# The recurrence of a two-layer block: gates one unit later, a third o buffer, spread partition sums, later output weights, first-visit keys scaled on ScalarE

## Chip, cores and metric

The kernel runs on one core of a Trainium2 chip. The metric is device time in microseconds (us) of one execution; a difference of about 0.2% is the smallest that a few runs of this kernel can tell from none.

## What is computed

Two layers of a diffusion-transformer block work on 1024 tokens (a grid of 16 x 64) and a context of 256 tokens, model width 1024. The first layer mixes by windowed means, the second by a bidirectional mLSTM; each mixer is followed by a gated convolutional feed-forward part. The change lies in the second layer's mixer, cut here to what matters:

```python
def _mlstm_chunkwise(q, k, v, ig, lf, state0, with_output):
    b = cumsum(lf)                          # per chunk
    w_end = exp(b_last - b + ig - g_max)
    c_chunk = einsum('bhcsk,bhcsv,bhcs->bhckv', k, v, w_end)     # key_values
    C_new = a * C + e * c_chunk                                   # carry
    s = einsum('bhctk,bhcsk->bhcts', q, k) * d_w                  # scores times decay
    num = einsum('bhcts,bhcsv->bhctv', s, v) + a_t * einsum('bhctk,bhckv->bhctv', q, c_prev)
    h = num / max(abs(den), exp(-m_t))
...
hs = h_f + flip(h_b)                        # forward and backward pass
yx = (sigmoid(o) * hs) @ w_out              # gates, then the output projection
```

There are eight heads, with keys of 64 and values of 128 channels. Everything is fp32; large matmuls are made of three products of high and low parts (fp32r).

## The kernel before, in words

All engines run programs written out by hand, ordered by semaphores; nothing is scheduled by a planner, so the order in the source is the order on each engine.

**Units.** The kernel uses chunks of 128 tokens: 2 of the context and 8 of the grid. A unit is one chunk in one direction; there are 20 (0 to 19), alternately forward and backward. Units 0 to 3 are of the context and only feed the state. Units 4 to 11 are the first visits of the grid's chunks, units 12 to 19 the second visits, which add the other direction's result (`second`). `carried` is 18: units 18 and 19 pass no state on. `again` is 12 to 17, and for these chunks the keys of the first visits (units 6 to 11) are kept in SBUF.

**A unit on TensorE.** In the loop over u from 4 to 19 TensorE issues `front(u + 1)` and `back(u)`. `front` turns the keys of the next unit into PSUM (`keys_turned`, L1768, only for first visits; the bank is free for the next keys once these have been weighed and kept) and makes the scores (L1798). `back(u)` makes the numerator from scores and values (L1857), turns the gated chunk of unit u - 2 (`turn`, L1885), adds the state's part (L1865) and makes the products of keys and values for the state (L1778). The sums of the modulation weights over the partitions (`chunk_columns`, L1898) are matmuls with one column: two chunks' worth after unit 17, six within unit 18, the rest after `turn(18)`. Then the output projection begins (L1122 to L1124), and `turn(19)` stands after its first eighth.

**The other engines in a unit.** VectorE: keys times their weights from PSUM (`kw`, L3819, first visits only), decay times scores (`dmat`, L3825), the new state (`carry`, L3872), the low part of the turned chunk (`g_lo`, L3880), and the division of the numerator (`dens`, `hs`, L3841 to L3861), in that order: front(u + 1), carry(u - 1), turned(u - 2), back(u). ScalarE: the decay's exponentials of unit u + 1, eight instructions (`dmat`, L2802); the copy of the keys to be kept (L2809) or, for units 12 to 17, the kept keys times their weights, head by head (L2819); the high part of the turned chunk of unit u - 2 (`g_hi`, L2792). GpSimd: mask added to the decay rows (`dmat`, L4169), decayed queries (`qa`, L4171), and from unit 14 on the gating of unit u - 2: `hs` times `och` (L4178). SyncE issues the loads: two iterations ahead the decay rows and query factors (L1011, L1014, broadcast to all partitions), the values (L997), and in iteration u the gate values `och` of unit u - 1 (L1023, `gates_in`), into two buffers. Between them stand the loads of the output projection's weights: `mo_raw` in iteration 14, parts of `raw` in iterations 15 and 16 (L1042, L725).

**Who waits for whom.** `turn(u - 2)` waits for the gating (`gated`) and for decay times scores of unit u + 1 (`sd_ready`), since it writes the bank from which VectorE reads the scores. The scores of unit u + 2 wait for `g_lo` of unit u - 2. The numerator of unit u waits bank by bank until VectorE has divided unit u - 1 (`hs_ready`). In `back(18)` the wait for the last state (`state_ready` of 4 * carried) stands ahead of the numerator.

**Earlier in the program.** Before the recurrence the same stretch of code projects o, q, k and v. For the first tile of o, ScalarE takes chunks out of PSUM into two `stage` buffers and stores each to DRAM from its own DMA queue (L2738, L2742). At the same time SyncE issues `res_c` (1 MB, L966), two weight tiles (1 MB each, L719) and two halves of modulation weights (0.5 MB each, L960).

## Time and profile before

| what | value |
|---|---|
| median of 3 runs | 2282.94 us (2279.64 to 2283.0) |
| profiled execution, its own time | 2282.74 us |
| its span, first to last instruction | 2280.9 us |
| TensorE matmul busy | 2201.2 us, 97% of the span |
| weight loads | 1834.1 us, 80% |
| VectorE | 1503.7 us, 66% |
| ScalarE | 1026.2 us, 45% |
| GpSimd | 1023.3 us, 45% |
| mean granted TensorE clock | 0.988 of full speed |

The busy time is a mean over stages. The profile's 40 slices show TensorE at nine tenths or more in nearly all of them. The recurrence of the grid's units runs from 1364 to 1486 us of the span, the output projection follows. In what follows all times are us from the span's start, in that one execution.

### The profile page before, as it was taken

The numbers are of one execution on the slowest core, as the hardware profiler recorded it, in microseconds if no ns is written. First come the engines' busy times: TensorE is split into PE (matmuls) and PEld (weight loads), VectorE is DVE, ScalarE is ACT, GpSimd is POOL, SyncE is SP. The second block draws the span as 40 slices with busy tenths as digits, with TensorE's granted clock in tenths as the row PEclk, the third lists the DMA queues.
The fourth block names the chain that finished last, engine by engine and source line by source line (L and its number), as shares of the span: only waits on it lengthen the run. The fifth ranks groups of instructions, "written<-read, shape, count | busy, mean of one in ns | idle before, by whom it ended". The sixth has DMA issues, their size and how long they took to land.

```text
span 2280.9 us, 35573 instructions
## 1 busy us (share of the span) xinstructions
PE 2201.2 (97%) x13206; PEld 1834.1 (80%) x13206; DVE 1503.7 (66%) x1993; ACT 1026.2 (45%) x1689; POOL 1023.3 (45%) x612
## 2 busy tenths in 40 slices
PE   7988999999999999999999999789999999999997
PEld 5647788888888889998899998767778888888885
DVE  5486666677798835455664727524676777888886
ACT  4654344444444455653433336423554444444443
POOL 0036677777610046661221025530497777771003
PEclk9999999999999999999999999899999999999998
DMA  8764432222292556543431358522212222228352
GB/s 342 252 231 166 157 134 87 83 83 83 84 340 75 167 212 225 191 166 130 124 117 65 107 152 258 175 74 74 75 65 84 82 80 81 108 95 291 129 175 102
DMA packets 123636, 326.33 MB, mean 143 GB/s; under 512 B 11376, under 2 KB 40816, under 8 KB 111216
## 3 DMA queue, kind: packets, MB, share of 16 engines
q1 hardware_dynamic: 105936, 299.35, 38.4%
q10 hardware_dynamic: 17568, 25.17, 3.0%
q8 instruction: 89, 1.46, 0.3%
q14 instruction: 43, 0.35, 0.0%
HBM read 269.82 MB, written 54.66 MB: 142 GB/s over the span
## 4 chain that ended last, share of the span: by engine, by line
PE 90%; DVE 3%; ACT 3%; DMA 2%; issue 1%; POOL 0%; SPq 0%; ACTq 0%; DVEq 0%; POOLq 0%
PE ps L1492 11%; PE ps L1494 11%; PE ps L1493 11%; PE ps L1122 7%; PE ps L1124 6%; PE ps L1123 6%; PE ps L1621 6%; PE ps L1622 6%; PE ps L1623 6%; PE ps L1665 3%; PE ps L1667 3%; PE ps L1666 3%; PE ps L1857 1%; PE ps L1260 1%; PE ps L1396 1%
## 5 line engine op out<-in xcount | busy, mean ns | idle before, releaser
L3225 DVE SCALAR_TENSOR_TENSOR acc<-ps,fcv,acc 128x945 f32<-128x945 f32 (+2 forms) x320 | 391.1, 1222 | 82.2 <-ACT acc L2385 49.6
L3986 POOL TENSOR_TENSOR w_lo<-raw,w_hi 128x2048 fp32r<-128x2048 f32 x36 | 169.5, 4708 | 375.8 <-ACT w_hi L2166 260.6
L4045 POOL TENSOR_TENSOR p_s_lo<-p_s_val,p_s_hi 128x512 fp32r<-128x512 f32 x160 | 242.8, 1527 | 117.1 <-ACT p_s_hi L2329 116.9
L1621 PE MATMUL ps<-da_hi,dw_hi 128*128 128x512 f32 x560 | 218.8, 391 | 0.0
L1622 PE MATMUL ps<-da_hi,dw_lo 128*128 128x512 f32 x560 | 218.1, 389 | 0.0
L1623 PE MATMUL ps<-da_lo,dw_hi 128*128 128x512 f32 x560 | 217.9, 389 | 0.0
L1665 PE MATMUL ps<-w_hi,hx_hi 128*128 128x256 f32 x512 | 145.8, 285 | 3.6 <-ACT stage L2738 3.5
L1666 PE MATMUL ps<-w_lo,hx_hi 128*128 128x256 f32 x512 | 144.9, 283 | 0.0
L1667 PE MATMUL ps<-w_hi,hx_lo 128*128 128x256 f32 x512 | 144.8, 283 | 0.0
L1621 PEld LDWEIGHTS ps<-da_hi,dw_hi 128*128 128x128 f32 x560 | 105.1, 188 | 23.2 <-issue 1.6
L1623 PEld LDWEIGHTS ps<-da_lo,dw_hi 128*128 128x128 f32 x560 | 105.1, 188 | 22.1
L2329 ACT ACTIVATE p_s_hi<-p_s_val 128x512 fp32r<-128x512 f32 x160 | 100.1, 626 | 50.0 <-POOL p_s_val L4036 49.9
L1622 PEld LDWEIGHTS ps<-da_hi,dw_lo 128*128 128x128 f32 x560 | 105.1, 188 | 21.6
L2385 ACT ACTIVATE acc<-ps,fcv 128x1024 f32<-128x1024 f32 x40 | 48.3, 1207 | 154.5 <-DVE ps L3262 148.9
L3669 DVE SCALAR_TENSOR_TENSOR acc_q<-ps,prm,acc_q 128x945 f32<-128x945 f32 (+2 forms) x64 | 78.2, 1222 | 48.9 <-ACT acc_q L2684 46.9
L1665 PEld LDWEIGHTS ps<-w_hi,hx_hi 128*128 128x128 f32 x512 | 98.2, 192 | 4.6 <-issue 2.3
L1122 PE MATMUL ps<-hc_hi,w_hi 128*128 128x256 f32 x352 | 100.2, 285 | 0.6 <-POOL w_lo L3986 0.6
L2166 ACT ACTIVATE w_hi<-raw 128x2048 fp32r<-128x2048 f32 (+1 forms) x62 | 95.3, 1545 | 12.0 <-DMA raw<-in_ffn_w 9.3
L1123 PE MATMUL ps<-hc_hi,w_lo 128*128 128x256 f32 x352 | 99.6, 283 | 0.0
L1124 PE MATMUL ps<-hc_lo,w_hi 128*128 128x256 f32 x352 | 99.5, 283 | 0.0
L1666 PEld LDWEIGHTS ps<-w_lo,hx_hi 128*128 128x128 f32 x512 | 98.2, 192 | 0.1
L1667 PEld LDWEIGHTS ps<-w_hi,hx_lo 128*128 128x128 f32 x512 | 98.2, 192 | 0.0
(523 smaller groups left out, 6499.8 us busy)
## 6 DMA issues: line engine op xcount, KB each, us to landing
f_raw<-in_ffn_w SPq DMA_DIRECT2D x25, 1024.0 KB, 5.0
modw<-in_modw SPq DMA_DIRECT2D x48, 512.0 KB, 8.3
raw<-in_ffn_w SPq DMA_DIRECT2D x23, 1024.0 KB, 5.0
a_scr<-fprod SPq DMA_DIRECT2D x40, 512.0 KB, 2.6
land_w<-in_ffn_w SPq DMA_DIRECT2D x40, 512.0 KB, 4.5
f_raw_b<-in_ffn_w SPq DMA_DIRECT2D x18, 1024.0 KB, 5.0
land_b<-a_scr SPq DMA_DIRECT2D x30, 512.0 KB, 5.4
raw<-in_mlstm_w SPq DMA_DIRECT2D x14, 1024.0 KB, 5.2
```

Source lines behind the costliest of these rows:

```text
L1122: pe.matmul(out, whi, hhi, start=first, stop=False)
L1492: pe.matmul(out, p_hi[p][:, ws], S.x(q, k)[0], start=(k == 0 and name in ("g1", "g2", "s1")), stop=False, skip_group_check=True)
L1493: pe.matmul(out, p_lo[p][:, ws], S.x(q, k)[0], start=False, stop=False, skip_group_check=True)
L1494: mm = pe.matmul(out, p_hi[p][:, ws], S.x(q, k)[1], start=False, stop=(k == KH - 1), skip_group_check=True)
L1621: pe.matmul(out, dw_hi[r][:, ws], da_hi[r][:], start=begins, stop=False, skip_group_check=True)
L1622: pe.matmul(out, dw_lo[r][:, ws], da_hi[r][:], start=False, stop=False, skip_group_check=True)
L1623: mm = pe.matmul(out, dw_hi[r][:, ws], da_lo[r][:], start=False, stop=(i == NK - 1), skip_group_check=True)
L1665: pe.matmul(out, hi[:, k, t0:t0 + CH], wcol(0, k, 0, 2), start=first, stop=False)
L1666: pe.matmul(out, hi[:, k, t0:t0 + CH], wcol(1, k, 0, 2), start=False, stop=False)
L1667: return pe.matmul(out, lo[:, k, t0:t0 + CH], wcol(0, k, 0, 2), start=False, stop=last)
L3225: dve.scalar_tensor_tensor(out, src, cv[:, t:t + 1], out, ALU.mult, ALU.add).then_inc(sem("tap_done"), 1)
L4045: pool.tensor_tensor(p_lo[p][:], src, p_hi[p][:].bitcast(F32), ALU.subtract).then_inc(S.sem("lo_in"), 1)
```

## The change

Seven edits, all in the second layer's mixer:

1. `och` is three buffers instead of two; SyncE issues the gate values of unit u in iteration u (before: of unit u - 1).
2. GpSimd gates unit u - 3 in iteration u instead of unit u - 2, and units 16 to 19 after the last mask.
3. The partition sums stand behind units 12 to 17, two chunks' worth (four matmuls in the program) each.
4. In `back(18)` TensorE waits for the last state only ahead of the state's part.
5. The loads of the output projection's weights move: `raw` parts from iterations 15 and 16 to 17 and 18, `mo_raw` from iteration 14 to behind the loop, once six units are gated. ScalarE waits for eight gatings before it makes `mo_hi`.
6. The keys of units 5 to 11 are weighed by ScalarE, head by head, instead of VectorE.
7. `res_c` is loaded one tile later, once four `stage` copies are done; the second weight tile and the two modulation halves stand behind it.

```diff
-        och = at("och", WORK, [P, 2, 1024])
+        och = [at(f"och{i}", o, [P, 1024]) for i, o in enumerate((WORK, WORK + 4096, WORK + 24576))]
...
-            sp.dma_start(res_c[:], xc_scr).then_inc(sem("resc_in"), 16)
             for t in range(2, len(MSEQ) + 2):
                 K = K_MIN + t
+                if t == 3:
+                    sp.wait_ge(sem("stage_ready"), 4)
+                    sp.dma_start(res_c[:], xc_scr).then_inc(sem("resc_in"), 16)
                 tile_in(K, a["mlstm_w"][t], K % 2)
...
-                    if i >= 2:
-                        sp.wait_ge(sem("gated"), i - 1)
-                    sp.dma_start(och[:, i % 2, :], o_scr[units[u][1] - 2]).then_inc(sem(f"o_in{i % 2}"), 16)
+                    if i >= 3:
+                        sp.wait_ge(sem("gated"), i - 2)
+                    sp.dma_start(och[i % 3][:], o_scr[units[u][1] - 2]).then_inc(sem(f"o_in{i % 3}"), 16)
...
-                if u == 14:
-                    sp.dma_start(mo_raw[:], a["mlstm_w"][len(MSEQ) + 2][:, 0:2048]).then_inc(sem("mo_in"), 16)
-                if u in (15, 16):
-                    tile_out(K_MOUT + u - 15, a["mlstm_w"][len(MSEQ) + u - 15], (K_MOUT + u - 15) % 2)
+                if u in (17, 18):
+                    tile_out(K_MOUT + u - 17, a["mlstm_w"][len(MSEQ) + u - 17], (K_MOUT + u - 17) % 2)
...
-                gates_in(u - 1)
-            gates_in(len(units) - 1)
+                gates_in(u)
+            sp.wait_ge(sem("gated"), 6)
+            sp.dma_start(mo_raw[:], a["mlstm_w"][len(MSEQ) + 2][:, 0:2048]).then_inc(sem("mo_in"), 16)
...
-                    pe.wait_ge(sem("state_ready"), 16 if i == 0 else 4 * carried if u == carried else 4 * (u - 1))
+                    pe.wait_ge(sem("state_ready"), 16 if i == 0 else 4 * (u - 1))
...
                     if u >= 2:
                         turn(u - 2)
+                    if u == carried:
+                        pe.wait_ge(sem("state_ready"), 4 * carried)
...
-                if u == carried - 1:
-                    chunk_columns(0, 2)
-                if u == carried:
-                    chunk_columns(2, 8)
+                if u in again:
+                    chunk_columns(2 * again.index(u), 2 * again.index(u) + 2)
             turn(len(units) - 2)
-            chunk_columns(8, HALVES // 2)
...
             def keep_keys(u):
+                if x_units[0] < u < again[0]:
+                    dr, n = units[u]
+                    act.wait_ge(sem("kt_done"), u + 1)
+                    act.wait_ge(sem("unit_done"), u - 1)
+                    for h in range(HEADS):
+                        c = 32 * dr + h
+                        ins = act.activation(kw[u % 2][:, 64 * h:64 * h + 64], ps[:, keys_bank(u), 64 * h:64 * h + 64], ACT.Copy,
+                                             scale=cols[:, n, 1, c:c + 1])
+                    ins.then_inc(sem("kw_ready"), 1)
                 if u in kept_index:
-                    act.wait_ge(sem("kw_ready"), u + 1)
...
+            act.wait_ge(sem("gated"), 8)
             act.wait_ge(sem("mo_in"), 16)
...
-                if u < again[0]:
+                if u <= x_units[0]:
                     dve.wait_ge(sem("kt_done"), u + 1)
...
-                for v in ([u - 2] if u < len(units) - 1 else [u - 2, u - 1, u]):
+                for v in ([u - 3] if u < len(units) - 1 else [u - 3, u - 2, u - 1, u]):
                     if v in sec_index:
                         i = sec_index[v]
                         pool.wait_ge(sem("hs_ready"), 3 * (x_index[v] + 1))
-                        pool.wait_ge(sem(f"o_in{i % 2}"), 16 * (i // 2 + 1))
-                        pool.tensor_tensor(hs[:, units[v][1] - 2, :], hs[:, units[v][1] - 2, :], och[:, i % 2, :], ALU.mult).then_inc(sem("gated"), 1)
+                        pool.wait_ge(*gate_landed(i))
+                        pool.tensor_tensor(hs[:, units[v][1] - 2, :], hs[:, units[v][1] - 2, :], och[i % 3][:], ALU.mult).then_inc(sem("gated"), 1)
```

GpSimd at units 14 to 16, before: `dmat` and `qa` of unit 14, then the gating of unit 12, and so on.

```order
158 L4169 TENSOR_TENSOR dmat<-dmat,masks 128x1024
159 L4171 TENSOR_TENSOR qa_168<-qa_168,q_x 128x512
160 L4169 TENSOR_TENSOR dmat<-dmat,masks 128x1024
161 L4171 TENSOR_TENSOR qa_169<-qa_169,q_x 128x512
162 L4178 TENSOR_TENSOR hs<-hs,och 128x1024
163 L4169 TENSOR_TENSOR dmat<-dmat,masks 128x1024
164 L4171 TENSOR_TENSOR qa_170<-qa_170,q_x 128x512
165 L4178 TENSOR_TENSOR hs<-hs,och 128x1024
```

The same place now; rows 160 and 161 are again unit 14.

```order
160 L4182 TENSOR_TENSOR dmat<-dmat,masks 128x1024
161 L4184 TENSOR_TENSOR qa_169<-qa_169,q_x 128x512
162 L4182 TENSOR_TENSOR dmat<-dmat,masks 128x1024
163 L4184 TENSOR_TENSOR qa_170<-qa_170,q_x 128x512
164 L4191 TENSOR_TENSOR hs<-hs,och_178 128x1024
165 L4182 TENSOR_TENSOR dmat<-dmat,masks 128x1024
```

The mask of unit 15 now stands ahead of the gating of unit 12, and so on for each later unit.

TensorE at the end of the recurrence, before: numerator, turn and state's part of units 18 and 19 with the partition sums between them (each `x2` row is one chunk's two matmuls).

```order
6281 L1898 MATMUL ps<-ones,msum_324 128x1 x2
6282 L1898 MATMUL ps<-ones,msum_325 128x1 x2
6283 L1798 MATMUL ps<-q_x,k_x 128x128 x8
6284 L1857 MATMUL ps<-vch_171,dmat 128x129 x8
6285 L1885 MATMUL ps<-ident,hs 128x128 x8
6286 L1865 MATMUL ps<-state,qa_169 128x129 x8
6287 L1898 MATMUL ps<-ones,msum_326 128x1 x2
6288 L1898 MATMUL ps<-ones,msum_327 128x1 x2
```

The same place now, from the last sums of unit 17 to the projection's first matmul.

```order
6291 L1905 MATMUL ps<-ones,msum_pair_325 128x1 x2
6292 L1905 MATMUL ps<-ones,modm_320 128x1 x2
6293 L1803 MATMUL ps<-q_x,k_x 128x128 x8
6294 L1862 MATMUL ps<-vch_171,dmat 128x129 x8
6295 L1892 MATMUL ps<-ident,hs 128x128 x8
6296 L1872 MATMUL ps<-state,qa_169 128x129 x8
6297 L1862 MATMUL ps<-vch_173,dmat 128x129 x8
6298 L1892 MATMUL ps<-ident,hs 128x128 x8
6299 L1872 MATMUL ps<-state,qa_170 128x129 x8
6300 L1892 MATMUL ps<-ident,hs 128x128 x8
6301 L1127 MATMUL ps<-g_hi,w_hi 128x512
```

Nothing stands between units 18 and 19 any more, nor behind `turn(18)`.

SyncE at the first tile of o, before: the loads that follow the first two modulation halves.

```order
241 L966 DMA res_c<-xc_scr 128x2048
242 L719 DMA raw<-in_mlstm_w 128x2048 x2
243 L960 DMA modm_318<-in_modw 128x1024
244 L960 DMA modm_319<-in_modw 128x1024
```

The same now; row 242 waits for four `stage` copies.

```order
241 L723 DMA raw<-in_mlstm_w 128x2048
242 L974 DMA res_c<-xc_scr 128x2048
243 L723 DMA raw<-in_mlstm_w 128x2048
244 L964 DMA modm_320<-in_modw 128x1024
245 L964 DMA modm_321<-in_modw 128x1024
```

One tile keeps its place; three loads stand behind `res_c`, and `res_c` behind the wait.

## Rows read from the trace of the kernel before

**Rows 1.** Busy time by stretch: start:end, length, each engine, clock, DMA share, GB/s.
```profile
1385.90:1414.25 28.35, 28.35 (x339) 24.98 (x340) 23.75 (x69) 17.14 (x57) 17.96 (x10) 1.00 0.82 231
1414.25:1455.00 40.75, 33.30 (x377) 29.20 (x378) 29.70 (x98) 24.14 (x82) 27.21 (x14) 0.96 0.97 288
1470.00:1480.00 10.00, 10.00 (x67) 9.71 (x67) 3.95 (x14) 3.88 (x3) 2.35 (x1) 0.67 0.01 2
```
**Rows 2.** Waits, 1350 to 1500: waiter <- releaser, us in total, times, longest.
```profile
POOL hs L4178 <- DMA och<-o_scr: 13.0, 4, 5.5
DVE dmat L3825 <- ACT dmat L2802: 8.0, 5, 3.4
```
**Rows 3.** Timeline of TensorE: start, us, operation, in brackets idle before.
```profile
1426.76 2.05 PE L1857 MATMUL ps<-vch,dmat 128*128 128x129 f32 x16
1432.41 1.67 PE L1885 MATMUL ps<-ident,hs 128*128 128x128 f32 x8 [3.60 <-DVE dmat L3825]
...
1449.79 1.06 PE L1885 MATMUL ps<-ident,hs 128*128 128x128 f32 x8 [1.04 <-issue]
...
1460.66 1.05 PE L1898 MATMUL ps<-ones,msum 128*128 128x1 f32 x8
1461.64 1.16 PE L1798 MATMUL ps<-q_x,k_x 64*128 64x128 f32 x16
1466.17 3.16 PE L1857 MATMUL ps<-vch,dmat 128*128 128x129 f32 x16 [3.37 <-DVE state L3872]
...
1475.16 3.79 PE L1857 MATMUL ps<-vch,dmat 128*128 128x129 f32 x16
...
1486.54 0.50 PE L1122 MATMUL ps<-g_hi,w_hi 128*128 128x512 f32 x1 [0.69 <-DVE g_lo L3880]
...
1501.92 0.66 PE L1260 MATMUL ps<-sq_p,ones 128*32 128x128 f32 x8 [5.07 <-ACT sq_p L2098]
```
**Rows 4.** Timeline of GpSimd at units 12 to 15.
```profile
1423.86 2.36 POOL L4178 TENSOR_TENSOR hs<-hs,och 128x1024 f32<-128x1024 f32 x1 [5.50 <-DMA och<-o_scr]
1426.17 2.36 POOL L4169 TENSOR_TENSOR dmat<-dmat,masks 128x1024 f32<-128x1024 f32 x1
```
**Rows 5.** Timeline of ScalarE: decays, kept keys, weighed keys.
```profile
1371.13 4.78 ACT L2802 ACTIVATE dmat<-dmat,cols 128x128 f32<-128x128 f32 x16
...
1388.70 0.60 ACT L2809 ACTIVATE kept_keys<-ps 128x512 f32<-128x512 f32 x1 [1.55 <-DVE kw L3819]
1389.19 2.43 ACT L2802 ACTIVATE dmat<-dmat,cols 128x128 f32<-128x128 f32 x8
...
1415.39 2.02 ACT L2819 ACTIVATE kw<-kept_keys,cols 128x64 f32<-128x64 f32 x8 [0.77 <-PE ps L1778]
```
**Rows 6.** DMA issues, 1410 to 1510: count, KB each, median us to landing.
```profile
qa<-query_scr SPq DMA_DIRECT2D x11, 128.0 KB, 6.5
...
raw<-in_mlstm_w SPq DMA_DIRECT2D x2, 512.0 KB, 10.5
```
**Rows 7.** Timeline of VectorE within one unit of the second visits.
```profile
1443.77 1.22 DVE L3880 TENSOR_TENSOR g_lo<-ps,g_hi 128x1024 fp32r<-128x1024 f32 x1 [1.22 <-ACT g_hi L2792]
...
1445.67 2.16 DVE L3853 SCALAR_TENSOR_TENSOR hs<-ps,dens,hs 128x128 f32<-128x128 f32 x8
1448.47 1.22 DVE L3825 TENSOR_TENSOR dmat<-dmat,ps 128x1024 f32<-128x1024 f32 x1 [0.64 <-ACT dmat L2802]
...
1451.95 1.22 DVE L3880 TENSOR_TENSOR g_lo<-ps,g_hi 128x1024 fp32r<-128x1024 f32 x1 [1.22 <-ACT g_hi L2792]
```
**Rows 8.** Timeline of three engines at the first tile of o.
```profile
1044.43 0.35 PE L1665 MATMUL ps<-w_hi,hx_hi 128*128 128x256 f32 x1 [1.95 <-ACT stage L2738]
...
1043.90 0.38 ACT L2738 ACTIVATE stage<-ps 128x256 f32<-128x256 f32 x1 [7.05 <-DMA o_scr<-stage]
...
1032.31 0.91 SPq L719 DMA_DIRECT2D raw<-in_mlstm_w  x2
```
**Rows 9.** One tile's instructions, `stage`: time from issue to landing of its stores.
```profile
DMA to landing us min/median/max: 1.8/2.2/8.8
```

4 lines of the change are left out of this document (3 added, 1 removed), and 2 rows, old and new, of the table shared.

## The prediction

> **What bounds the kernel now.** I read the page first: TensorE is busy for 97% of the span of 2280.9 us, so only its idle time and its slow time can be won, some 80 us in all. The busy time by stretch splits the recurrence in two. In the first visits TensorE is busy for all of 28.35 us (units 7 to 11, 5.79 us each with keys to turn, 5.20 without), while the 16 DMA engines are 0.82 taken; from 1414 to 1455 it is busy for 33.3 of 40.75 us and the DMA engines are 0.97 taken [rows 1]. Then the waits: GpSimd waited 13.0 us for gate values and VectorE 8.0 us for ScalarE's decays [rows 2]. In the timelines both are one chain, seen once in full: the gating of unit 12 starts at 1423.86, 5.50 us late, the mask of unit 15 behind it at 1426.17 [rows 4], and TensorE stands 3.60 us before `turn(12)` at 1432.41 [rows 3]. At the end it waits 3.37 us for the last state and then runs slowly: the numerator of unit 19 takes 3.79 us where that of unit 14 took 2.05 [rows 3], with the granted clock at 0.67 in that stretch [rows 1], between the levels of 1.2 and 2.4 GHz. The projection starts at 1486.54 [rows 3].
>
> **The change, part by part.** I work out when the projection starts; after it both kernels do the same.
>
> *Keys on ScalarE.* VectorE is rid of one instruction a unit, but TensorE has no gap there [rows 1], so this gains nothing. ScalarE gets eight instructions, 2.02 us as for the kept keys, beside a decay of 2.43 and a copy of 0.60 [rows 5]: 5.05 us of 5.79. These read PSUM, where the row reads SBUF. At the start the keys of unit 5 stand behind its decay: 1371.13 + 4.78 / 2 + 2.02 = 1375.5, where TensorE wants them at 1375.3 (two units of 5.79 ahead of 1386.9, where a unit starts). With the semaphore's delay: +0.35 us. Bounds: 0, and what 0.60 us for each of the eight would make of it, the copy's time for eight times the columns (a rival below).
>
> *Partition sums.* Eight records took 0.98 us (1460.66 to 1461.64 [rows 3]). Behind units 12 and 13, where TensorE has no gap, they cost 2 x 0.98 = +1.96. Behind 14 to 17 they fall into waiting, as follows.
>
> *Unit 14.* `turn(12)` needs the gate values, the gating, and decay times scores of unit 15. The values are issued one iteration (5.2 us) earlier and no `mo_raw` lies beside them; the mask of unit 15 no longer stands behind the gating. Its rows had landed by 1426.17, when its mask began without a wait [rows 4]; at the median of 6.5 us from issue [rows 6] they landed by about 1422, since SyncE issues them once the numerator of unit 11 is done, at 1414.25 (where the first stretch of rows 1 ends). Mask 2.36, queries 1.3 and gating 2.36 end at 1428 (or 1432.2 by the late bound, +1.1); decay and product are earlier. The numerator of unit 14 starts at 1426.76 + 1.96 + 0.35 = 1429.1 and takes 1.98; so `turn(12)` is at 1431.05, not 1432.41. The 3.60 us are gone, the 2.31 added in front remain.
>
> *Units 15 to 17: a loop takes over.* From `turn` to the end of `g_lo` takes 1449.79 to 1451.95 + 1.22 = 1453.17, 3.38 us [rows 3, 7]. Then VectorE divides: from 1444.99 to 1447.83, 2.84 us; then decay times scores, 1.22, and small gaps of 0.1 bring the next `turn` 4.15 us after `g_lo` [rows 7]. The period is 3.38 + 4.15 = 7.55 us. Before it was 8.18 (`g_lo` at 1443.77 and 1451.95), of which 0.64 was the wait for the decay [rows 7]; that goes. TensorE's own work is 5.20, a turn of 1.07 and 0.98 for the sums, 7.25, so the sums are hidden here. GpSimd's work (6.0) fits too. DMA: 28.35 x 0.82 / 5 = 4.65 us a unit without gate values; the second stretch took 39.5 us for 5.5 such units and 5.2 MB of other loads, so 2.7 us a MB and 1.4 for a unit's gate values [rows 1]; 6.05 a unit, 7.5 where a part of `raw` comes. The DMA engines follow, just.
>
> `g_lo` of unit 12 ends at 1434.4, that of 15 three periods later at 1457.1; the scores of unit 19 start 0.8 later (7.25 less scores 1.09 and numerator 1.98 is 4.18 after the turn, less 3.38), 1457.9, where they started at 1461.64: **-3.7**, with all sums done.
>
> *Units 18 and 19.* The numerator of 18 no longer waits for the state (3.37). `turn(16)` 1457.1 + 4.15 = 1461.25; `g_lo` 1464.6; now the numerator of 19 waits for the division of 18 (its first heads 1.7 us after `g_lo`): 1466.35, `turn(17)` 1468.3, `g_lo` 1471.7, `turn(18)` 1471.8, `g_lo` 1475.2. **Projection at 1475.3, -11.2 us.** The low part of its first weights (VectorE, behind `g_lo` of 17) fits between. The new wait of 2.9 us at unit 19 stands where 24 records of sums stood.
>
> *Clock.* That wait is shorter than the two (3.60, 3.37) behind which the trace shows slow matmuls: after the first only a turn (1.67 for 1.06), after the second a numerator (3.16 for 2.05) as well [rows 3]. Bounds: 0 to +2.4 (a numerator at 3.7 and a turn at 1.7). I take the middle, **+1.1**: the length of the wait is near theirs, but only two blocks can be caught.
>
> *Output weights.* The parts of `raw` are issued around 1435 and 1443, at 10.5 us to land [rows 6]; wanted at 1463 and later. `mo_raw` goes out once unit 17 is gated, about 1462, and lands before 1475; it is wanted behind `turned(19)`, some 20 us after its issue. Covered; if not, each us late is a us lost. The stall of 5.07 us in the projection's second eighth, where TensorE waits for ScalarE's work behind `mo_hi` [rows 3], is not touched.
>
> *`res_c`.* TensorE waited 1.95 us at 1044.43 for a `stage` copy, which waited 7.05 for a store to land; median is 2.2 [rows 8, 9]. Ahead of the store SyncE had issued `res_c` and two tiles, up to 1032.31 + 0.91 [rows 8]. Now one tile is there, so the store lands before the copy is wanted: **-1.95**. The later loads meet the next stores, which TensorE needs 6 us later; bounds 0 and -1.95, and I take the full gain since the wait has that slack. `res_c` itself was used 50 us later. The rule against it: the Trainium skill, "DMA: Bandwidth & Descriptors", section "Queues, rings and completion order", says that each DMA engine takes turns between the queues packet by packet. By that ScalarE's store would not stand behind SyncE's backlog, this part would give 0 and the time would be 1.95 us longer; the 7.05 against 2.2 speaks for the backlog.
>
> Sum: -11.2 (with +0.35 and +1.96 inside) + 1.1 - 1.95 = -12.0. The profiled execution took 2282.74 in all, 1.8 around the span, and lies 0.2 below the median of 2282.94; so 2282.94 - 12 = **2271.0**.
>
> **Rivals.**
> *Half of it.* Something of the chain mask, decay, product stays late, because the DMA engines at 6 to 7.5 us a unit fall behind: then unit 14 keeps its 3.60 and the period its 8.18 (3 x 0.64), together 5.5 to 6 of the 12. For it: 6.5 and 10.5 us to landing with the engines full [rows 6]. Against: two iterations of lead, and 2 MB gone. Time 2277.
> *Given back in the projection.* Its start is earlier, but `mo_raw` or the modulation columns come late, or the stall behind `mo_hi` grows by as much. If all 10.1 us of the recurrence go, only `res_c` is left: 2281. Against: the loads land over 10 us ahead of their use, by the above.
> *ScalarE binds the first visits.* At 0.60 us for each of the eight, a unit takes 4.8 + 2.43 + 0.60 = 7.8 us instead of 5.79, six times, and unit 5's keys come 2.8 us later: +15, time 2271 + 15 = 2286. It costs from 0.34 us each, and eats the gain from 0.55. Against: 2.02 for eight [rows 5].
> *The clock falls within the second visits, slower than before.* Now TensorE has three short waits in each of units 15 to 17 and one-column matmuls between. If the clock stayed at its lower level there, a unit would take about 5 us more (numerator 3.7 for 2.0, and all others alike), from unit 14 to 19 +25: 2271 + 25 = 2296. It decides once 2.4 units run so. Against: the second stretch had waits of over 1 us in each unit and was granted 0.96 [rows 1]; eight such records stood ahead of scores at full speed, 1.16 [rows 3]. The Trainium skill, "TensorE: Matmul & The Clock Gate", section "A second HAM failure mode: psum-queue depth-cycling", tells of a kernel whose frequent short idles between groups made the clock swing; that speaks for this rival, and the trace so far does not show it.
>
> **How the numbers follow.** Forecast (2268 to 2274): 0.66. Half: 0.17. Given back: 0.06. ScalarE binds: 0.04. Clock: 0.03. What I have not seen and leaves the time as it is: 0.04. The difference that a measurement can tell is 0.2%, 4.6 us. Faster: the first two, and a part of the third, 0.85; same: 0.10; slower: 0.05. The range goes from 2268 (no clock loss, and a run as far below its median as one of those shown) to 2278, which takes in the half.
>
> **What would show it.** Right: no idle before `turn(12)`; `g_lo` every 7.5 to 7.6 us; scores of 19 about 3.7 us earlier relative to unit 12; idle of about 3 us before the numerator of 19, released by VectorE's `hs`; all L1905 sums by then; the projection 11 to 13 us earlier in the span; no wait near 1044. Wrong: ScalarE over 5.8 us a unit in the first visits; GpSimd waiting for `och` or rows from unit 15 on; a granted clock under 0.9 from 1430 to 1460; idle above 5 us in the projection's second eighth.

## The result, and the profile of the kernel after

The changed kernel takes 2268.25 us (median of 4 runs, 2266.68 to 2268.69); the kernel before 2281.29 (4 runs, 2279.26 to 2283.0). The ratio is 0.994, 95% interval 0.9924 to 0.9955: 13.0 us less, where I had forecast 12.0 less and 2271.0. The time lies 2.75 below the forecast and 0.25 above the lower end of the range that I gave (2268 to 2278). 1.65 of the 2.75 is the reference: the three runs that I started from had their median at 2282.94, and a fourth at 2279.26 moved it to 2281.29. Some 1.1 is the change itself. A second comparison (run e11 below, 5 runs against 9) gives 2268.17 against 2279.99, ratio 0.9947 (0.9932 to 0.9962), 11.8 less. So the forecast gain of 12.0 lies between the two measured ones, 13.0 and 11.8; that its parts were not all right is shown further down.

Of the profiled execution (2268.69 us, span 2266.6) I read the timeline of TensorE at the places of [rows 3].

```profile
1037.35 0.39 ACT L2742 ACTIVATE stage<-ps 128x256 f32<-128x256 f32 x1 [1.47 <-DMA o_scr<-stage]
...
1044.60 0.38 ACT L2742 ACTIVATE stage<-ps 128x256 f32<-128x256 f32 x1 [3.24 <-DMA o_scr<-stage]
...
1047.75 0.39 ACT L2742 ACTIVATE stage<-ps 128x256 f32<-128x256 f32 x1 [2.77 <-DMA o_scr<-stage]
...
1050.22 0.39 ACT L2742 ACTIVATE stage<-ps 128x256 f32<-128x256 f32 x1 [2.08 <-DMA o_scr<-stage]
...
1051.62 0.32 PE L1139 MATMUL ps<-sq_c,ones 128*32 128x64 f32 x8 [0.92 <-ACT sq_c L2060]
```

These are the copies of the first tile of o [rows 8], in ScalarE's timeline, and the one wait in TensorE's. The 7.05 us before the third copy are 1.47, and the 1.95 us before TensorE's matmul are gone. The copies behind it wait instead (3.24, 2.77, 2.08; the waits at the same place before were at most 1.15), since `res_c` and its followers are now issued from 1038.60 on. So ScalarE reaches the squares `sq_c` only 0.24 us earlier than before, counted from the first matmul of o (29.87 for 30.11), while TensorE comes 1.95 earlier, and it stands 0.92 us where it did not stand before.

TensorE in the recurrence, lines of numerator (L1862), turn (L1892) and projection (L1127):

```profile
1426.70 2.05 PE L1862 MATMUL ps<-vch,dmat 128*128 128x129 f32 x16
1428.59 1.04 PE L1892 MATMUL ps<-ident,hs 128*128 128x128 f32 x8
...
1436.01 1.06 PE L1892 MATMUL ps<-ident,hs 128*128 128x128 f32 x8 [0.20 <-issue]
...
1458.33 0.85 PE L1892 MATMUL ps<-ident,hs 128*128 128x128 f32 x6 [0.20 <-issue]
...
1463.40 2.07 PE L1862 MATMUL ps<-vch,dmat 128*128 128x129 f32 x16 [2.91 <-DVE hs L3866]
...
1472.25 0.60 PE L1127 MATMUL ps<-g_hi,w_hi 128*128 128x512 f32 x1 [2.37 <-DVE g_lo L3893]
...
1487.34 0.66 PE L1265 MATMUL ps<-sq_p,ones 128*32 128x128 f32 x8 [4.81 <-ACT sq_p L2102]
```

Against [rows 3]: no idle before `turn(12)` (3.60 before), a turn every 7.44 us (8.17 from `turn(13)` to `turn(14)` before, its start 1441.62 and 1449.79), one wait of 2.91 before the numerator of unit 19 and that numerator at 2.07 (3.79), the stall in the projection as it was (4.81 for 5.07). Busy time by stretch, columns as in [rows 1]:

```profile
1383.94:1412.29 28.35, 28.35 (x338) 24.98 (x340) 21.38 (x65) 23.91 (x90) 18.34 (x11) 1.00 0.75 222
1412.29:1453.04 40.75, 40.16 (x458) 36.19 (x460) 32.79 (x106) 26.05 (x86) 33.15 (x17) 1.00 1.02 302
```

The first visits are as full as before, and ScalarE has gone from 17.14 to 23.91 us in them. In the second stretch (as long as that of [rows 1], from the same point of the loop) TensorE is busy for 40.16 us instead of 33.30, in full. GpSimd waits no more for gate values. In place of the waits of [rows 2] there are these (behind the colon: us in total, times, longest), counted here from 1340 to 1500:

```profile
POOL dmat L4182 <- DMA qa<-query_scr: 66.1, 14, 29.7
...
POOL hs L4191 <- DVE hs L3866: 17.7, 3, 8.1
...
DVE dmat L3838 <- ACT dmat L2806: 5.1, 2, 4.5
```

Counted alike, GpSimd waited 59.4 us in 10 times for queries before; the longest, 29.7 us now and 28.8 before, is one wait ahead of the loop.

**A table by stretch.** Executions of one kernel differ by up to 5 us before the changed part begins, so I compare lengths between the same instructions: the first matmul of the first tile of o, the turned keys of unit 5, with which the loop of the units begins (the texts written ahead of the runs e10 to e13 call the same instruction the keys of unit 6), `turn(12)`, and the projection's first matmul. These are the first two in the kernel before:

```profile
1022.16 0.28 PE L1665 MATMUL ps<-w_hi,hx_hi 128*128 128x256 f32 x1
...
1369.50 0.66 PE L1768 MATMUL ps<-ident,k_x 128*128 128x128 f32 x4 [0.47 <-ACT stage L2738]
```

and in the kernel after:

```profile
1021.19 0.28 PE L1670 MATMUL ps<-w_hi,hx_hi 128*128 128x256 f32 x1
...
1367.54 0.66 PE L1773 MATMUL ps<-ident,k_x 128*128 128x128 f32 x4 [0.47 <-ACT stage L2742]
```

| us | o to keys of 5 | keys of 5 to turn(12) | keys of 5 to projection | numerator of 19 | all, us |
|---|---|---|---|---|---|
| before | 347.34 | 62.91 | 117.04 | 3.79 | 2282.74 |
| after | 346.35 | 61.05 | 104.71 | 2.07 | 2268.69 |
| e1: edit 7 alone | 345.59 | 63.98 | 117.49 | 3.79 | 2280.97 |
| e2: without edit 6 | 345.87 | 61.05 | 106.09 | 2.62 | 2267.83 |
| e3: sums in the waits | 346.08 | 59.39 | 104.51 | 3.53 | 2268.28 |
| e4: without edit 4 | 345.70 | 61.05 | 112.77 | 3.78 | 2274.24 |
| e5: without edit 2 | 345.90 | 61.55 | 107.79 | 3.78 | 2273.75 |
| e6: two buffers | 345.75 | 61.05 | 104.72 | 2.07 | 2268.85 |
| e7: edit 5 alone | 348.81 | 63.63 | 113.93 | 2.06 | 2278.08 |
| e8: edit 2 alone | 348.70 | 59.39 | 107.76 | 2.07 | 2274.92 |
| e9: projection's order | 345.97 | 61.05 | 106.22 | 2.74 | 2262.54 |
| e10: e9 and e3 | 345.68 | 59.40 | 104.69 | 3.46 | 2261.38 |
| e11: after, again | 346.25 | 61.05 | 106.09 | 2.61 | 2268.17 |
| e12: without edit 3 | 345.79 | 59.39 | 104.43 | 3.42 | 2266.93 |
| e13: after, gap filled | 345.89 | 61.05 | 104.70 | 2.16 | 2267.06 |
| e14: e9, gaps filled | 345.78 | 61.05 | 104.70 | 2.16 | 2260.56 |
| e15: e10, gaps filled | 346.39 | 59.38 | 103.06 | 2.16 | 2259.92 |

The last column is one execution for before, after and e1 to e8, a median of 4 or 5 from e9 on. The lengths are of one execution each. Before against after: 1.0 less up to the keys, 12.3 less in the recurrence, and nothing from the projection's start to the end (794.36 and 794.35, although the stall there is 0.3 shorter). A further 0.97 of the span's 14.3 lies ahead of the first matmul of o, where nothing was changed: such starts lie between 1019.11 (e7) and 1024.47 (e5). So the last column of two single executions can differ by 5 us without a cause in the edits, and I read e1 to e8 by the lengths.

### The profile page after: what moved, and what is told of

Its sections match the earlier page's. It is cut to its first block, busy times and chain, and to the rows that moved or that the text cites. A ratio compares the mean times of both kernels' runs of the same rounds, so it can differ in the third digit from the quotient of the medians.

```text
span 2266.6 us, 35623 instructions
## 1 busy us (share of the span) xinstructions
PE 2195.4 (97%) x13206; PEld 1828.9 (81%) x13206; DVE 1503.4 (66%) x1986; ACT 1036.8 (46%) x1745; POOL 1023.8 (45%) x612
## 3 DMA queue, kind: packets, MB, share of 16 engines
q8 instruction: 89, 1.46, 0.3%
## 4 chain that ended last, share of the span: by engine, by line
PE 91%; DVE 3%; ACT 3%; DMA 2%; issue 1%; POOL 0%; ACTq 0%; SPq 0%; DVEq 0%
PE ps L1497 11%; PE ps L1499 11%; PE ps L1498 11%; PE ps L1127 7%; PE ps L1128 6%; PE ps L1129 6%; PE ps L1626 6%; PE ps L1627 6%; PE ps L1628 6%; PE ps L1670 3%; PE ps L1672 3%; PE ps L1671 3%; PE ps L1862 1%; PE ps L1265 1%; PE ps L1401 1%
## 5 line engine op out<-in xcount | busy, mean ns | idle before, releaser
L1127 PE MATMUL ps<-hc_hi,w_hi 128*128 128x256 f32 x352 | 100.2, 285 | 0.7 <-POOL w_lo L3999 0.7
L4259 POOL TENSOR_TENSOR y_x<-y_x,res_x 128x512 f32<-128x512 f32 x12 | 17.1, 1451 | 180.7 <-DVE y_x L3964 180.7
```

Of the source, the lines that this page charges most:

```text
L1127: pe.matmul(out, whi, hhi, start=first, stop=False)
```

## The experiments

**e1, edit 7 alone**, in the kernel before.

```diff
-            sp.dma_start(res_c[:], xc_scr).then_inc(sem("resc_in"), 16)
             for t in range(2, len(MSEQ) + 2):
+                if t == 3:
+                    sp.wait_ge(sem("stage_ready"), 4)
+                    sp.dma_start(res_c[:], xc_scr).then_inc(sem("resc_in"), 16)
```

> The kernel before with edit 7 alone (res_c, one weight tile and two modulation halves behind four stage copies). Backlog theory: ScalarE's second pair of stage copies no longer waits 7.05 us for a store, TensorE's wait of 1.95 us near 1044 is gone, and everything from there on starts 1.95 us earlier: the projection at 1484.6, the time about 2281 beside 2282.9. Rival, the DMA engines take turns between the queues: store and wait stay as they were, the projection at 1486.5.

The wait near 1044 is gone, and o to keys is 1.75 shorter. The recurrence kept its length (117.49), but the wait before `turn(12)` grew to 4.67. So the backlog on the other queue did hold the store, and part of the gain is given back behind the loads in their new place: TensorE waits 0.36 us for the squares `sq_c` here too.

**e2, edit 6 undone**: VectorE weighs the keys again.

```diff
-                if x_units[0] < u < again[0]:
-                    ...
-                        ins = act.activation(kw[u % 2][:, 64 * h:64 * h + 64], ps[:, keys_bank(u), ...], ACT.Copy, scale=...)
...
-                if u <= x_units[0]:
+                if u < again[0]:
                     dve.wait_ge(sem("kt_done"), u + 1)
```

> The changed kernel with edit 6 undone: VectorE weighs the keys of units 5 to 11 again. Theory that the edit gives nothing: TensorE is packed in the first visits either way, units of 5.79 us, the projection at 1472.2 within 0.2 us, time as the changed kernel's. Rival, it was VectorE's relief that removed a late division or a late product at the turn from first to second visits: a wait of 0.3 to 1 us shows before a numerator of units 11 to 13, and the projection is later by as much.

Up to `turn(12)` the two are equal to 0.01 us. Edit 6 brings and costs nothing that can be seen. The difference to the projection is the numerator of unit 19, which ran slowly in this execution.

**e3, the sums only where TensorE waits**: none behind units 12 and 13, the missing four chunks' worth between units 18 and 19.

```diff
-                if u in again:
-                    chunk_columns(2 * again.index(u), 2 * again.index(u) + 2)
+                if u in again[2:]:
+                    chunk_columns(2 * again.index(u) - 4, 2 * again.index(u) - 2)
+                if u == carried:
+                    chunk_columns(8, HALVES // 2)
```

> The changed kernel with the partition sums of units 12 and 13 taken away from there: two chunks' worth behind each of units 14 to 17, the last four behind unit 18, where TensorE waits 2.91 us for VectorE. Theory of the waits: 1.96 us of sums leave the packed units 12 and 13 and vanish in the wait; the projection starts 1.9 to 2.0 us earlier, 1470.3. Clock theory: a wait of 1 us instead of 2.91 keeps the clock as it is, no effect. Rival, DMA or decays had no slack in units 12 to 14 and the 1.96 us covered them: a wait of up to 2 us comes before turn(12) and nothing is gained.

`turn(12)` comes 1.66 us earlier, but the projection only 0.2. In TensorE's timeline:

```profile
1458.64 1.50 PE L1905 MATMUL ps<-ones,msum_pair 128*128 128x1 f32 x12
1460.00 0.58 PE L1905 MATMUL ps<-ones,modm 128*128 128x1 f32 x4
1461.62 3.53 PE L1862 MATMUL ps<-vch,dmat 128*128 128x129 f32 x16 [1.03 <-DVE hs L3868]
```

The gap has shrunk from 2.91 to 1.03 us, and the numerator behind it is slower than in the kernel after, 3.53 for 2.07. The numerator starts 1.65 us earlier (counted from the keys of unit 5) and takes 1.46 longer: what was won ahead is lost at the lower clock.

**e4, edit 4 undone**: in unit 18 the wait for the last state stands ahead of the numerator again.

```diff
-                    pe.wait_ge(sem("state_ready"), 16 if i == 0 else 4 * (u - 1))
+                    pe.wait_ge(sem("state_ready"), 16 if i == 0 else 4 * carried if u == carried else 4 * (u - 1))
...
-                    if u == carried:
-                        pe.wait_ge(sem("state_ready"), 4 * carried)
```

> The changed kernel with edit 4 undone: in back(18) the wait for the last state stands ahead of the numerator again. Theory: the numerator of 18 starts at carry's end (about 1459.3) instead of 1456.1, turn(16) at 1461.2 instead of 1458.3, the projection 2.9 us later, 1475.2, if the clock stays. Clock theory: a wait of about 3.2 us is as long as those behind which the kernel before ran slowly (3.37, 3.60), longer than the 2.91 that stayed at full speed; then numerators take over 3 us, and the projection is 4 to 6 us later.

```profile
1457.94 3.78 PE L1862 MATMUL ps<-vch,dmat 128*128 128x129 f32 x16 [3.37 <-DVE state L3883]
...
1467.34 3.78 PE L1862 MATMUL ps<-vch,dmat 128*128 128x129 f32 x16 [2.91 <-DVE hs L3864]
```

Two waits and two slow numerators: the recurrence is 8.1 us longer than in the profile of after, more than either theory had. Counted from the keys, the numerator of 18 starts 3.4 us later, that of 19 5.5 later, the projection 8.1 later. The last 2.5 are the numerator and turn of unit 19 at the lower clock, which e5 shows with edit 4 in place (2.6). So some 5.5 us belong to edit 4, the largest share of any edit that was undone alone: 3.4 of waiting and 2.1 of lower clock behind it.

**e5, edit 2 undone**: GpSimd gates unit u - 2 again.

```diff
-                for v in ([u - 3] if u < len(units) - 1 else [u - 3, u - 2, u - 1, u]):
+                for v in ([u - 2] if u < len(units) - 1 else [u - 2, u - 1, u]):
```

> The kernel after with edit 2 undone: GpSimd gates unit u-2 in iteration u again, so the mask and the decayed queries of unit 15 stand behind the gating of unit 12 (edits 1, 3 to 7 stay). Theory 1 (the 3.60 us before turn(12) were the late gate values; once they are loaded an iteration earlier the order on GpSimd hardly matters): the gating starts without a DMA wait once unit 12 is divided; its hs ends at about 1421 in the kernel after, gating 2.36, mask 2.36, decay 2.43, product 1.22 would end at 1429.5, so turn(12) waits 1 us at most, the period stays at 7.4 to 7.5, and the projection starts within 0.5 us of 1472.3. Theory 2 (the order on GpSimd was half of the gain, as my prediction told it): turn(12) waits 2 us or more on the decay, the period is over 7.8, the projection starts at 1474 or later.

```profile
1431.92 1.06 PE L1892 MATMUL ps<-ident,hs 128*128 128x128 f32 x8 [0.33 <-POOL hs L4191]
...
1439.36 1.06 PE L1892 MATMUL ps<-ident,hs 128*128 128x128 f32 x8 [0.20 <-issue]
```

GpSimd's mask of unit 15 in the same run, and VectorE's one wait for a decay between 1400 and 1500:

```profile
1425.69 2.35 POOL L4182 TENSOR_TENSOR dmat<-dmat,masks 128x1024 f32<-128x1024 f32 x1
...
DVE dmat L3838 <- ACT dmat L2806: 1.1, 1, 1.1
```

`turn(12)` waits 0.33 us, and the period behind it is 7.44. The bracket names GpSimd's gating, but that is the gating of unit 13, which `turn(12)` does not need; that of unit 12 had ended at 1425.73. What `turn(12)` waited for is again the chain mask, decay, product: the mask of unit 15 at 1425.69, straight behind the gating, ScalarE's decay at 1428.07 behind it, and VectorE's product, 1.08 us late, from 1430.55 to 1431.77. So in time the run is as theory 1 has it, half a us to `turn(12)`, but the wait is small because the sums of edit 3 stand ahead of it: `turn(12)` comes 61.55 us after the keys, where e8 and e12, with the other order on GpSimd and no sums there, have 59.39. What the order is worth with the loads moved and without those sums was not run; the two lengths put it near 2.2 us. The other 2.6 us of the longer way to the projection are the numerator and turn of unit 19 at the lower clock.

**e6, gate values as if there were two buffers.**

```diff
-                    if i >= 3:
-                        sp.wait_ge(sem("gated"), i - 2)
+                    if i >= 2:
+                        sp.wait_ge(sem("gated"), i - 1)
```

> The kernel after, but the gate values of unit v wait until all but one of the earlier ones are used up, as with two buffers (edit 1 half undone: still issued an iteration earlier in SyncE's order). SyncE is in order, so with gating at u-3 this load waits for the gating of unit v-2, and what stands behind it (decay rows and queries of the coming units) waits as well. Theory 1 (the third buffer is what allows edit 2): GpSimd waits for rows or gate values by 1 us or more in units 15 to 17, the period rises over 7.7, the projection starts 1 to 4 us after 1472.3. Theory 2 (the lead of two iterations has room for it): same period, projection within 0.3 us of 1472.3.

No difference in the recurrence (61.05 to `turn(12)`, 104.72 in all). The third buffer is not needed.

**e7, edit 5's loads alone**, in the kernel before.

```diff
-                if u == 14:
-                    sp.dma_start(mo_raw[:], ...)
-                if u in (15, 16):
-                    tile_out(K_MOUT + u - 15, ...)
+                if u in (17, 18):
+                    tile_out(K_MOUT + u - 17, ...)
...
             gates_in(len(units) - 1)
+            sp.wait_ge(sem("gated"), 6)
+            sp.dma_start(mo_raw[:], ...)
```

> The kernel before with edit 5's loads alone: mo_raw behind the loop, the raw parts in iterations 17 and 18. Theory 1 (the 1 MB of mo_raw and the parts of raw delayed the gate values through the full DMA engines): the wait of GpSimd for the gate values of unit 12 shrinks from 5.50 to about 3 us or less (1 MB at 2.7 us), the 3.60 us before turn(12) to 1 or less; the projection starts 2 to 4 us before 1486.54. Theory 2 (the gate values come late since they are issued late, behind the broadcasts of the next unit): the 5.50 and the 3.60 stay within 1 us, the projection starts within 1 us of 1486.54.

```profile
1423.01 2.36 POOL L4178 TENSOR_TENSOR hs<-hs,och 128x1024 f32<-128x1024 f32 x1 [6.14 <-DMA och<-o_scr]
...
1431.55 1.94 PE L1885 MATMUL ps<-ident,hs 128*128 128x128 f32 x8 [4.32 <-DVE dmat L3825]
```

Half of each theory. At unit 12 nothing is won (6.14 and 4.32 where it was 5.50 and 3.60), and in the kernel before SyncE had issued those gate values at 1416.44, ahead of `mo_raw` at 1417.13: they were late because they were issued late. The later ones landed in time: from `turn(12)` to `turn(15)` it is 23.78 us instead of 25.13 (1432.41 to 1457.54). The rest of the 3.1 us, 2.5, is the numerator and turn of unit 19, which ran at full clock here, and that right behind the same one-column sums as in the kernel before:

```profile
1470.02 2.39 PE L1898 MATMUL ps<-ones,msum 128*128 128x1 f32 x20
1472.27 0.58 PE L1898 MATMUL ps<-ones,msum_pair 128*128 128x1 f32 x4
1473.00 2.06 PE L1857 MATMUL ps<-vch,dmat 128*128 128x129 f32 x16
```

**e8, edit 2 alone**, in the kernel before.

```diff
-                for v in ([u - 2] if u < len(units) - 1 else [u - 2, u - 1, u]):
+                for v in ([u - 3] if u < len(units) - 1 else [u - 3, u - 2, u - 1, u]):
```

> The kernel before with edit 2 alone: GpSimd gates unit u-3 in iteration u, two buffers, gate values issued late. Theory 1 (the chain mask, decay, product behind the gating made the wait): the mask of unit 15 runs by 1423, decay and product no longer hold turn(12), which then waits only for the gating, 1423.9 or later + 2.36 = 1426.2 to 1428.7; the 3.60 us shrink to 0 to 1. But SyncE, which waits for a gating before it refills a buffer, is held up one unit more, so gate values and rows come late from unit 15 on and the projection is 0 to 3 us earlier than 1486.54. Theory 2 (the late gate values are the cause whatever the order): turn(12) still waits 2.5 us or more.

No wait before `turn(12)`, period 7.44, 9.3 of the 12.3 us of the recurrence, by one line; some 2.5 of the 9.3 are the numerator and turn of unit 19, which ran at full clock in this execution (2.07 for 3.79), as in e7. Even so it is more than theory 1 expected: SyncE was not held up, GpSimd's masks waited 2.52, 1.25 and 1.20 us for rows, and ScalarE waited at most 0.8 us for a mask. Gate values that came late did no harm here with an iteration between them and their use. So the order on GpSimd takes the wait before `turn(12)` away with the loads as they were; the loads without it (e5) shorten the same wait, with the sums of edit 3 covering most of what is left. Behind `turn(12)` either gives the period of 7.44.

**e9, another order in the projection**, in the kernel after: ScalarE squares the first eighth before it makes the next high parts, and TensorE sums these squares later.

```diff
-                        if k == 2 and d >= 1:
+                        if k == (6 if (h, d) == (0, 1) else 2) and d >= 1:
                             half_sums("p", 2 + h, d - 1)
...
+            copy_out(0, 0)
             for n in range(4):
                 plain_high(0, n)
-            for d in range(KT):
+            for d in range(1, KT):
                 copy_out(0, d)
```

> The kernel after with two steps of the output projection in another order: ScalarE takes the first eighth out of PSUM and squares it before it makes the four high parts of the next weights, and TensorE sums those squares behind the seventh of the eight channel blocks of the second eighth instead of behind the third. In the kernel after, TensorE stands 4.81 us before these sums (released by ScalarE's sq_p) and its next 12 matmuls take 0.63 us instead of 0.39. Theory 1 (ScalarE's order alone makes the stall, and the slow matmuls follow from the idle): both go, 4.8 + 12 x 0.2 = 7.2 us less from the projection's start to the second half's first squares; 2261 us in all. Theory 2 (another wait takes its place: the squares wait for GpSimd's w_lo, which ends at 1482.97, or the later high parts hold up GpSimd): part of it stays, 2263 to 2267. Theory 3 (all given back later): 2268.

2262.54 us, ratio to before 0.9919 (0.9904 to 0.9934), 5.6 us less than the kernel after beside it. The stall is gone:

```profile
1487.96 0.42 PE L1265 MATMUL ps<-sq_p,ones 128*32 128x128 f32 x8
```

From the projection's start to the end of the program it is 787.3 us instead of 793.4 in e11 (794.4 in the first profile), 6.1 to 7.1 less, near the 7.2 of theory 1. Which of the two moves, ScalarE's or TensorE's, does it was not taken apart.

**e10, e9 with the sums of e3.**

> As the run above, and with the sums of the run e3 (none behind units 12 and 13, the missing ones between units 18 and 19). In e3 the end of the recurrence was reached only 0.2 us earlier (104.51 against 104.71 us from the keys of unit 6), since the numerator of unit 19 ran slowly. Theory 1 (the clock at unit 19 is a matter of chance, whatever stands in the gap): this run is 0 to 3 us faster than the one above, about 2260. Theory 2 (one-column matmuls in the gap bring the slow clock every time, a true wait of 2.9 us only sometimes): same as the run above within 1 us, the numerator of unit 19 slow again.

2261.38 us, ratio 0.9918 (0.9903 to 0.9933), within the scatter of e9. The numerator of unit 19 is slow again (3.46 behind 1.04 of idle time), as theory 2 has it for this run; its "every time" does not hold, since the numerators of e7 and e8 behind such sums took 2.06 and 2.07.

**e11, the kernel after again.**

> The kernel after, unchanged, as the measure for the runs beside it: 2268 us, ratio 0.994. Theory 1 (the clock at unit 19 is a matter of chance): the numerator of unit 19 behind its 2.9 us of idle time may be fast (2.07) or slow (up to 3.8) in this execution; from the keys of unit 6 to the projection 104.7 us if fast, 107.7 if slow. Theory 2 (2.9 us of idle are always short enough): 104.7 again.

```profile
1462.49 2.61 PE L1862 MATMUL ps<-vch,dmat 128*128 128x129 f32 x16 [2.91 <-DVE hs L3866]
1464.90 1.91 PE L1892 MATMUL ps<-ident,hs 128*128 128x128 f32 x8
```

The same code behind the same 2.91 us of idle time, and here numerator and turn run slowly where the first profile had 2.07 and 1.07: 1.4 us more to the projection. The clock is a matter of the execution.

**e12, edit 3 undone**: the sums as before.

```diff
-                if u in again:
-                    chunk_columns(2 * again.index(u), 2 * again.index(u) + 2)
+                if u == carried - 1:
+                    chunk_columns(0, 2)
+                if u == carried:
+                    chunk_columns(2, 8)
             turn(len(units) - 2)
+            chunk_columns(8, HALVES // 2)
```

> The kernel after with edit 3 undone: the partition sums stand as before (two chunks' worth behind unit 17, six between units 18 and 19, the rest behind turn(18)). Theory 1 (the sums behind units 12 and 13 are pure cost, 1.96 us, the others are free in either place): from the keys of unit 6 to turn(12) 59.4 us instead of 61.05, period 7.44, no idle before the numerator of unit 19, whose clock decides: 102.8 us to the projection if it stays up, about 106 if it falls; in all 2266 or 2269. Theory 2 (the sums keep TensorE's clock up in units 14 to 17): without them granted clock under 0.95 there and a period over 7.5, 2270 or more.

```profile
1458.79 2.39 PE L1905 MATMUL ps<-ones,msum 128*128 128x1 f32 x20
1461.04 0.80 PE L1905 MATMUL ps<-ones,msum_pair 128*128 128x1 f32 x4
1461.77 3.42 PE L1862 MATMUL ps<-vch,dmat 128*128 128x129 f32 x16
```

Same as the kernel after or a little better (0.9941, interval 0.9926 to 0.9957, against 0.9947). 24 one-column matmuls fill the gap without a rest, and the numerator still takes 3.42. Edit 3 brings nothing.

**e13, the gap filled**: the kernel after with 20 transposes of 128 columns ahead of the numerator of unit 19, into a bank that nobody reads (work is added, none left out).

```diff
+            def fill(n0):
+                for j in range(n0):
+                    pe.transpose(ps[:, 7, P * (j % 3):P * (j % 3) + P], k_tile(2, j % 4), ident[:])
...
+                    if u == carried + 1:
+                        fill(20)
                     for g, heads in enumerate(by_bank):
```

> The kernel after, with 20 transposes of 128 columns whose results nobody reads, put into the wait ahead of the numerator of unit 19 (some 2.6 of the 2.91 us; they add work and leave none out). Theory 1 (the clock at unit 19 falls because TensorE stands there; whether it does is decided by chance at 2.91 us): with the gap filled the numerator takes 2.05 every time, from the keys of unit 6 to the projection 104.7 us or less (106.1 and more in four of six profiles with the gap open), 2267 us in all. Theory 2 (the clock falls there for another reason, such as the waits from unit 15 on taken together): the numerator still takes 2.6 us or more, 2268 or more.

```profile
1458.86 2.40 PE L1845 MATMUL ps<-ident,k_x 128*128 128x128 f32 x20
1461.74 2.16 PE L1869 MATMUL ps<-vch,dmat 128*128 128x129 f32 x16 [0.48 <-DVE hs L3873]
```

The numerator runs at full clock, and in e14 and e15 too (2.16 each). The time, 2267.06 (2265.8 to 2269.79), cannot be told from that of the kernel after: the stake is 1 us. By chance, three profiles of three would be fast about once in forty times, if four in fourteen are (the table without e13 to e15).

**e14, e9 with three gaps filled** (20 ahead of the numerator of 19, 8 ahead of `turn(18)`, 16 behind it).

> The run e9 with such transposes in three waits: 20 ahead of the numerator of unit 19, 8 ahead of turn(18), 16 behind it, ahead of the projection. Theory 1: numerator, turn and the projection's first nine matmuls (0.63 us each in the kernel after, 0.40 at full clock) all run at full clock, 1.4 + 9 x 0.2 = 3.2 us less than e9, 2259 to 2260. Theory 2: same as e9, 2262.5.

```profile
1468.02 1.91 PE L1845 MATMUL ps<-ident,k_x 128*128 128x128 f32 x16
1470.56 0.50 PE L1127 MATMUL ps<-g_hi,w_hi 128*128 128x512 f32 x1 [0.63 <-DVE g_lo L3903]
...
1476.77 1.09 PE L1899 MATMUL ps<-ident,hs 128*128 128x128 f32 x8 [0.43 <-POOL hs L4201]
...
1483.58 0.43 PE L1265 MATMUL ps<-sq_p,ones 128*32 128x128 f32 x8 [0.93 <-ACT sq_p L2111]
```

The projection's first matmuls take 0.40 instead of 0.63, but TensorE then meets `turn(19)` 0.43 and the squares 0.93 too early: of the 1.8 us hoped for there, 0.4 is left by these waits, and 0.2 by the length from the projection's start to the end (787.0 for 787.3 in e9), less than two executions of one kernel differ by. 2260.56 us, ratio 0.9913 (0.99 to 0.9927), 2.0 less than e9 was in its own comparison; the intervals of the two overlap.

**e15, e10 with gaps filled**: the last four chunks' sums and four transposes stand behind `turn(18)`, 20 and 8 transposes ahead as in e14. Against e14, behind the loop:

```diff
             fill(8)
             turn(len(units) - 2)
-            fill(16)
+            chunk_columns(8, HALVES // 2)
+            fill(4)
```

> As the run above, but no sums behind units 12 and 13 (1.66 us less to turn(12)); the last four chunks' sums (one-column matmuls) stand behind turn(18) with four transposes, where the run above has sixteen transposes. Theory 1 (one-column matmuls do not keep the clock up, transposes do): numerator of unit 19 at 2.05, the projection's first matmuls slow again (0.63); 1.66 less than the run above and up to 1.8 more: 2259 to 2260. Theory 2 (any matmul keeps it up): all fast, 2257.5 to 2258.

```profile
1468.54 1.40 PE L1912 MATMUL ps<-ones,msum_pair 128*128 128x1 f32 x12
1469.80 0.58 PE L1912 MATMUL ps<-ones,modm 128*128 128x1 f32 x4
1470.24 0.64 PE L1845 MATMUL ps<-ident,k_x 128*128 128x128 f32 x4
1471.08 0.50 PE L1127 MATMUL ps<-g_hi,w_hi 128*128 128x512 f32 x1 [0.20 <-DVE g_lo L3904]
1471.89 0.60 PE L1127 MATMUL ps<-g_hi,w_hi 128*128 128x512 f32 x1
```

2259.92 us, ratio 0.9909 (0.9894 to 0.9924), 20.4 less than before: the lowest median, not to be told from e14. With the clock kept at unit 19, what the sums behind units 12 and 13 cost does come back: 103.06 us to the projection instead of 104.70. TensorE rested for only 0.20 us ahead of the projection, and yet its matmuls are slow from the second on (0.60, then 0.63), where e14, with transposes in place of the sums, has 0.40. Theory 1, on one profile of each.

## Why the prediction was right or wrong

**The chain before `turn(12)`: right.** Idle 3.60 gone; keys of 5 to `turn(12)` took 61.05, forecast 61.55 (1431.05 - 1369.50). The chain mask, decay, product that I named is what binds in e5 too. But I told it as the sum of three edits, and it is not: e8 has it by the order on GpSimd alone, and e7 shows that the loads of the output weights had no part in it, since these gate values had been issued ahead of `mo_raw`. e5 has most of it by the earlier gate values, with the sums covering the rest.

**The sums behind 12 and 13: right** (+1.96 forecast). 1.66 came back when they were moved away (e3, e12), since `turn(12)` then waits a little. What I missed is that they buy nothing: without them at units 12 and 13, the gap at unit 19 holds them, at the same end time. Only with transposes in that gap (e15) does their cost of 1.66 show in the end time as well.

**Keys of unit 5: the term was over by 0.35.** I took 2.02 us for ScalarE's eight, the row from SBUF, and my working (1375.5 against 1375.3) gave 0.2 of the 0.35; for the semaphore's delay that made up the rest I had no row. From PSUM the eight took 1.70 to 1.79, and the keys of units 5 and 6 stood 5.78 us apart, as before. One row of them:

```profile
1385.59 1.75 ACT L2817 ACTIVATE kw<-ps,cols 128x64 f32<-128x64 f32 x8
```

**The period: right in mechanism, over in size.** 7.44 for 7.55, four times, 0.44 us. (My two terms, 3.38 and 4.15, add up to 7.53.) From `turn` to the end of `g_lo` it is 3.37 us, as forecast (3.38). From there (1438.16 + 1.22) to the next `turn` at 1443.45 it is 4.07, not 4.15: the small gaps of 0.1 that I had put between VectorE's steps are not there. VectorE's timeline behind that `g_lo`:

```profile
1440.06 2.16 DVE L3866 SCALAR_TENSOR_TENSOR hs<-ps,dens,hs 128x128 f32<-128x128 f32 x8
1442.13 1.21 DVE L3838 TENSOR_TENSOR dmat<-dmat,ps 128x1024 f32<-128x1024 f32 x1
1445.60 1.23 DVE L3893 TENSOR_TENSOR g_lo<-ps,g_hi 128x1024 fp32r<-128x1024 f32 x1 [1.22 <-ACT g_hi L2796]
```

**Units 18 and 19: right.** The new wait was forecast at 2.9 and released by `hs`; it is 2.91. From `turn(16)` to the projection it took 13.92, forecast 14.05 without the clock's share.

**The clock, +1.1: 0 in the first profile, right on the average.** In the six profiles that have the open gap of 2.91 us (after, e2, e5, e6, e9, e11) the way to the projection is longer than 104.71 by 0, 1.38, 2.58 (e5, less the 0.5 at `turn(12)`), 0.01, 1.51 and 1.38: 1.14 on average. That it is the standing that brings the lower clock was only argued before; e13, e14 and e15 are the evidence for it: with matmuls of 128 columns in the gap the numerator took 2.16 in three of three.

**`res_c`, -1.95: the step that failed.** "The later loads meet the next stores, which TensorE needs 6 us later": I looked for the next reader of PSUM, and put the new place of the loads at nothing. The first to suffer was ScalarE's own queue of work: three copies waited 8.1 us together, the squares behind them came only 0.24 us earlier, and TensorE stood 0.92 us there. All fourteen profiles with edit 7 have this wait, of 0.36 to 0.92 us; the three without it have none. So of the 1.95 us of waiting, 1.0 to 1.6 are saved, and 1.0 in the pair of profiles.

A second thing, which I had not priced, works the other way. Behind the old wait the matmuls ran slowly in two of the three profiles that have it (e7 and e8; 0.41 us where 0.28 is usual):

```profile
1041.37 0.36 PE L1665 MATMUL ps<-w_hi,hx_hi 128*128 128x256 f32 x1 [1.94 <-ACT stage L2738]
...
1042.49 0.41 PE L1665 MATMUL ps<-w_hi,hx_hi 128*128 128x256 f32 x1
```

The granted clock was 0.91 in the 20 us around that wait in both, and TensorE was busy for 344.7 and 344.8 us from o to the keys instead of 343.3; none of the fourteen with edit 7 has it (343.1 to 343.4, granted 1.00). So the length from o to keys is 347.3, 348.8 and 348.7 without edit 7 and 345.9 on average with it, 2.4 less: some 1.3 of waiting and 1.1 of clock. That this comes near the 1.95 is luck.

I had weighed a rule against this step. The Trainium skill, "DMA: Bandwidth & Descriptors", section "Queues, rings and completion order", says that each DMA engine takes turns between the queues packet by packet. From it I had worked out that the store would not stand behind another queue's backlog. The wait of 7.05 that fell to 1.47 when the backlog was moved (1.36 in e1, with this edit alone) speaks against its giving 0 here.

**Together.** Recurrence -10.1 forecast, -12.3 in the profile, -11.2 with the clock's average. Without the clock's share that is -11.2 forecast and -12.3 measured: `turn(12)` 0.5 earlier, the period's 0.46, and 0.13 in units 18 and 19. `res_c` -1.95 forecast, -1.0 in the profile, -2.4 against the mean of the three; from the projection's start on, nothing. In the one pair of profiles the two errors have opposite signs, which is why the sum looks better than its parts. The rest of the miss in the absolute time is the reference: medians of the kernel before were 2282.94, 2281.29, 2279.99 and 2280.33, and I gave a range of 3 us downwards from a median of three.

**The rivals.** None came. Half of it: GpSimd found its gate values (waits gone), though the DMA engines were full. Given back in the projection: the stall shrank by 0.3, and from the projection's start to the end both took 794.4. ScalarE in the first visits: 5.79 us a unit, unchanged. The clock within the second visits: granted 1.00 from 1412 to 1453 in spite of a 0.20 us wait and one-column matmuls in each unit. The Trainium skill, "TensorE: Matmul & The Clock Gate", section "A second HAM failure mode: psum-queue depth-cycling", tells of a kernel in which short idles between groups made the clock swing; that does not show here.

What stays open: why the same 2.91 us cost nothing in two executions and 1.4 to 2.6 us in four, why the one-column sums ahead of the numerator of unit 19 left it fast in two profiles (e7, e8) and slow in five (before, e1, e3, e10, e12), and what edit 1, the earlier gate values, is worth alone, which was not run.
